# Three products ahead of RWKV-7's recurrent rounds, made by GpSimd instead of VectorE

## The reference, cut to what matters

```
def wkv7_scan(r, w, k, v, kk, a):
    def step(state, xs_t):
        r_t, w_t, k_t, v_t, kk_t, a_t = xs_t
        sa = jnp.einsum('bhvk,bhk->bhv', state, -kk_t)
        state = (state * w_t[:, :, None, :] + sa[..., None] * (kk_t * a_t)[:, :, None, :]
                 + v_t[..., None] * k_t[:, :, None, :])
        return state, jnp.einsum('bhvk,bhk->bhv', state, r_t)
...
def rwkv7_group(p, mu, w0, w2, a0, a2, g2, k_k, k_a, r_k, ln_w, ln_b):
...
    y = wkv7_scan(r_h, heads(decay), k_h, v_h, kk, heads(a))
...
    bonus = jnp.sum(r_h * k_h * r_k, axis=-1, keepdims=True) * v_h
    return (y + bonus.reshape(b, s, RW_WIDTH)) * gate
```

## Time and profile before

| | |
|---|---|
| median of 3 executions | 2797.43 us (2796.68 to 2800.03) |
| the profiled execution | 2797.85 us, of which the span of the trace is 2796.0 us |
| PE, PEld busy | 2748.7 us (98%), 2380.8 us (85%) |
| DVE busy | 1913.8 us (68%) |
| ACT busy | 1399.0 us (50%) |
| POOL busy | 106.9 us (4%) |
| granted TensorE clock, mean | 0.998 |

### The profile page before, as it was taken

How to read it: one execution, slowest core, us unless ns; L and a number is a source line. 1 busy time by engine, 2 the same in 40 slices (tenths; PEclk the granted TensorE clock), 3 DMA queues, 4 the chain that set the end, 5 groups by cost and what they waited for, 6 DMA issues and landing times.

```text
span 2796.0 us, 46874 instructions
## 1 busy us (share of the span) xinstructions
PE 2748.7 (98%) x17930; PEld 2380.8 (85%) x17930; DVE 1913.8 (68%) x2378; ACT 1399.0 (50%) x1805; POOL 106.9 (4%) x122
## 2 busy tenths in 40 slices
PE   9999999999999999999999999989999999999998
PEld 8888888888888888888887888788988888888886
DVE  7898887768656556566687665955876566575664
ACT  6545557566434444344567545635664344344444
POOL 0000000151000000000000000030200000000000
PEclk9999999999999999999999999999999999999999
DMA  7555554766666665665465444402645666656654
GB/s 245 184 184 181 158 171 154 231 194 195 190 194 188 192 192 188 195 188 190 150 194 160 128 129 121 147 22 96 198 153 184 198 190 188 195 187 191 192 188 151
DMA packets 415239, 487.83 MB, mean 174 GB/s; under 512 B 14961, under 2 KB 346737, under 8 KB 415073
## 3 DMA queue, kind: packets, MB, share of 16 engines
q1 hardware_dynamic: 413216, 478.55, 54.7%
q0 software_dynamic: 1856, 6.98, 0.7%
HBM read 482.33 MB, written 3.15 MB: 174 GB/s over the span
## 4 chain that ended last, share of the span: by engine, by line
PE 89%; DVE 6%; ACT 3%; issue 2%; DMA 0%; ACTq 0%; SPq 0%; DVEq 0%
PE pg L514 36%; PE pg L521 20%; PE pg L465 17%; PE pg L470 8%; DVE lo L370 1%; PE pg L476 1%; DVE work L924 1%; ACT hi L329 1%; PE p L1687 1%; PE p L1988 1%; DVE xa L782 0%; PE p L2001 0%; DVE dnc L1354 0%; PE p L1243 0%; DVE work L902 0%
## 5 line engine op out<-in xcount | busy, mean ns | idle before, releaser
L370 DVE TENSOR_TENSOR lo<-raw,hi 128x1024 fp32r<-128x1024 f32 x895 | 1081.9, 1228 | 683.9 <-ACT hi L329 680.3
L329 ACT ACTIVATE hi<-raw 128x1024 fp32r<-128x1024 f32 (+1 forms) x894 | 935.6, 1056 | 1118.7 <-PE pg L521 654.3
L514 PE MATMUL pg<-xa,hi 128*128 128x512 f32 x4144 | 1048.1, 395 | 2.4 <-DVE work L417 1.0
L514 PEld LDWEIGHTS pg<-xa,hi 128*128 128x128 f32 x4144 | 745.8, 189 | 140.6 <-issue 2.0
L521 PEld LDWEIGHTS pg<-xa,lo 128*128 128x128 f32 x4208 | 573.3, 190 | 50.0 <-DVE lo L370 10.0
L521 PE MATMUL pg<-xa,lo 128*128 128x256 f32 x4208 | 588.5, 283 | 4.7 <-DVE lo L370 4.7
L465 PE MATMUL pg<-hi,xb 128*128 128x512 f32 x2048 | 506.0, 389 | 0.0
L465 PEld LDWEIGHTS pg<-hi,xb 128*128 128x128 f32 x2048 | 383.9, 188 | 79.4
L470 PE MATMUL pg<-lo,xb 128*128 128x512 f32 x1024 | 273.7, 389 | 0.0
L470 PEld LDWEIGHTS pg<-lo,xb 128*128 128x128 f32 x1024 | 192.2, 188 | 39.9
L514 PE MATMUL pg<-xb,hi 128*128 128x512 f32 x896 | 226.1, 394 | 0.1
(11 more groups left out here) (428 smaller groups left out, 1673.3 us busy)
## 6 DMA issues: line engine op xcount, KB each, us to landing
raw<-w_in SPq DMA_DIRECT2D x264, 512.0 KB, 4.5
raw<-ffn_w SPq DMA_DIRECT2D x256, 512.0 KB, 3.8
raw<-w_up SPq DMA_DIRECT2D x128, 512.0 KB, 3.9
raw<-w_down SPq DMA_DIRECT2D x128, 512.0 KB, 4.5
raw<-w_o SPq DMA_DIRECT2D x32, 512.0 KB, 4.8
raw<-w_out SPq DMA_DIRECT2D x32, 512.0 KB, 4.6
raw<-w_sb_out SPq DMA_DIRECT2D x16, 512.0 KB, 4.9
raw<-w_conv_out SPq DMA_DIRECT2D x16, 512.0 KB, 4.7
```

The source lines that it names most:

```text
L329: nc.scalar.activation(hi[:, slot, :, 0:g.tiles * P], raw[:, slot, :, 0:g.tiles * P], ACT.Copy).then_inc(hi_ready, 1)
L370: nc.vector.tensor_tensor(lo[:, slot, :, wide_], raw[:, slot, :, wide_], hi[:, slot, :, wide_].bitcast(F32), ALU.subtract).then_inc(lo_rea ...
L514: nc.tensor.matmul(pg[:, par, t, :], lhsT=hi[:, slot, k, c:c + P], rhs=g.x[:, kk, :], start=(j == 0 and k == 0), stop=False)
```

## The change

Three DVE instructions become POOL instructions with the same operands: alpha, rho (both 128 x 2048) and bn (128 x 1536). They stand in a new function `rwp_pool`, ahead of `rw_pool(pool, 0)` in POOL's program. alpha waits for "ba" and for ep; rho waits for "beta" too, since it overwrites what beta reads; bn waits for the summed bonus and for the third block of v. The readers wait for POOL instead: PE before the product `mat(pe, "ba", 0)`, DVE before it copies masks (`rw_cut`) over a part of ep, and DVE in the last round before it adds to bn. The steps of DVE beside the other slabs stay where they are.

```
@@ rwp_pe
             RP.act.wait(pe, "kt")
+            RP.pool.wait(pe, "rho")
             mat(pe, "ba", 0)
@@ rwp_dve
-            RP.act.wait(dve, "ep")
             RP.dve.wait(dve, "ba")
-            RP.dve.done(nc.vector.tensor_tensor(jc(rw_ar[:, 0]), jc(rw_kk[:, :, :]), ctok(rw_ep, 0), ALU.mult), "alpha")
+            RP.act.wait(dve, "em")
             yield
             RP.dve.done(nc.vector.tensor_tensor(jc(rw_beta[:, :, :]), jc(rw_a[:, :, :]), ctok(rw_em, 1), ALU.mult), "beta")
...
+            RP.act.wait(dve, "ep")
             dve_link(nc.vector.tensor_tensor(fac, rw_ep[:, 0:16:2, P], rw_em[:, 1:16:2, 0], ALU.mult))
...
-            RP.dve.done(nc.vector.tensor_tensor(jc(rw_ar[:, 1]), jc(rw_r), ctok(rw_ep, 1), ALU.mult), "rho")
             yield from skip(6)
-            RP.act.wait(dve, "bonus")
-            dve.wait_ge(v_shifted, 3)
-            RP.dve.done(nc.vector.tensor_tensor(rw_bn[:, 0:6], rw_bn[:, 0:6], rw_v[:, 0:6], ALU.mult), "bn")
+            RP.pool.wait(dve, "rho")
+        def rwp_pool(pool):
+            RP.dve.wait(pool, "ba")
+            RP.act.wait(pool, "ep")
+            RP.pool.done(nc.gpsimd.tensor_tensor(jc(rw_ar[:, 0]), jc(rw_kk[:, :, :]), ctok(rw_ep, 0), ALU.mult), "alpha")
+            pool.wait_ge(r_shifted, 4)
+            RP.dve.wait(pool, "beta")
+            RP.pool.done(nc.gpsimd.tensor_tensor(jc(rw_ar[:, 1]), jc(rw_r), ctok(rw_ep, 1), ALU.mult), "rho")
+            RP.act.wait(pool, "bonus")
+            pool.wait_ge(v_shifted, 3)
+            RP.pool.done(nc.gpsimd.tensor_tensor(rw_bn[:, 0:6], rw_bn[:, 0:6], rw_v[:, 0:6], ALU.mult), "bn")
```

More of the change, by code:

```diff
@@ L1742, in build_program @@
         RP = Trio("rwp", ["wa0", "wa1", "kk", "bonus", "bt", "vt01", "vt23", "b2"],
-                  ["scan0", "scan1", "sc", "k", "kk", "ba", "alpha", "beta", "bonus", "kappa", "rho", "bn", "bn3"],
+                  ["scan0", "scan1", "sc", "k", "kk", "ba", "beta", "bonus", "kappa", "bn3"],
                   ["tanh", "wa0", "wa1", "kkr", "sq", "kf", "max", "ln", "root", "em", "ep", "bonus", "bt", "kt", "vt01",
-                   "vt23", "b2", "k2"])
+                   "vt23", "b2", "k2"], ["alpha", "rho", "bn"])
         lora_in = sem("lora_in")
@@ L2221, in rw_pe @@
             if not r:
-                RP.dve.wait(pe, "rho")
+                RP.pool.wait(pe, "rho")
             beside = tail_pe(pe, r - 1) if r else beside_first_pe(pe)
@@ L2356, in rw_dve @@
                 state_dve(dve, r, 2)
+                RP.pool.wait(dve, "bn")
                 for j in range(8):
@@ L2628, in _ @@
                 pool.dma_start(rw_lw[h][64:P, :], a["rw_a2_2"][:, 512 * h:512 * h + 512]).then_inc(lora_in, 16)
+            rwp_pool(pool)
             for r in range(4):
```

## The result

| | before | changed |
|---|---|---|
| median | 2797.72 us (2794.67 to 2800.03, 15 executions) | 2802.89 us (2800.56 to 2806.57, 15 executions) |
| span of the profiled execution | 2796.0 us | 2800.7 us |
| ratio | | 1.0021, 95% interval 1.0013 to 1.0028 |

The changed kernel is 5.2 us slower in the median, 5.9 us by the ratio. The forecast was 2804.1 us, 6.7 us slower than the 2797.4 us that the prediction started from.

What follows compares the result with a forecast made beforehand. DVE was taken to bound the 25.3 us stretch after 1785.7, PE the rest. Terms 1.6 + 4.5 - 0.3 + 0.9 = 6.7 us slower gave a median of 2804.1 us, range 2799.5 to 2808.5.

Steps and rivals of the forecast that it cites:

- low end: Lower edge of the forecast's own range, 2803.0 us: holds of 4.2 us and the clock staying up.
- The bound: In the 25.3 us after 1785.7, DVE's gapless chain sets PE's pace; alpha and rho off it would gain 2.5 us.
- The hold: POOL's alpha and rho each keep DVE's two-SBUF-input instructions (L425, first L1916) waiting 4.5 us; L422, reading PSUM, runs.
- The sum: Whole kernel: L425 1.6, rho's hold 4.5, rho's step -0.3, clock 0.9, together 6.7 us slower.
- Rho's own step: Rho's 2.20 us leave DVE behind the chain's last split, shortening only PE's next wait: 0.3 us gained.
- The clock: PE's idle before its matmuls of 1800.13 grows from 1.25 to 5.8 us, and the granted clock falls: 0.9 us.
- third rival: POOL gets in one instruction earlier, with a second long idle for the clock: 2804.8 to 2806.5 us; 12%.
- bn: Ahead of round 0, DVE's 4.3 us of idle time covers POOL's bn hold of at most 3.4 us: nothing.
- DVE isn't held: Rival: DVE runs beside POOL's products and its chain gets 2.5 us shorter, 2794.9 us; 15%.
- POOL gets its turn only in part: Rival: alpha holds DVE, but rho waits for a gap in DVE's work; 1.3 us slower, 2798.7, up to 2801.5; 15%.
- One instruction earlier: Rival: POOL's alpha goes ahead of the split of 1784.78, costing 2.3 instead of 1.6 us, 2804.8 to 2806.5; 12%.
- POOL is slower on these tiles: Rival: ep is read in pieces of 128 columns, the examples in 256, so POOL takes longer: 2806 to 2809.5 us; 8%.

Runs made afterwards that it cites:

- alpha alone: Only the alpha product on POOL, rho and bn left on DVE, against the kernel before: 2797.94 against 2797.52 us, ratio 1.0003; stretch from kk to round 0 +1.08 us.
- The fills: Against the changed kernel, POOL fills the places of alpha and rho with zeros, bn on DVE: 2794.01 us, kernel before 2797.52; stretch -2.39 us.
- late order on DVE: Against the kernel before, alpha and rho stay on DVE but five and one steps later, nothing moved to POOL: 2795.23 against 2797.26 us; stretch -2.38 us.
- late on POOL: Against the changed kernel, alpha on POOL waits for the last split of g_rv, bn on DVE: 2801.53 us, kernel before 2797.26; stretch +2.54 us.
- rho alone: Only the rho product on POOL, alpha and bn left on DVE, against the kernel before: 2803.90 against 2797.52 us, ratio 1.0021; stretch +5.52 us.
- eight pieces: Against the changed kernel, alpha and rho each as eight POOL instructions of 256 columns, bn on DVE: 2804.35 us, kernel before 2797.26; stretch +5.69 us.
- late on DVE once more: Repeat of the kernel with alpha and rho later on DVE, against the kernel before: 2795.53 against 2797.80 us, ratio 0.9993; stretch -2.39 us.
- POOL multiplies by zero: Against the changed kernel, POOL multiplies kk and kk*a by zero, one SBUF input, bn on DVE: 2803.31 us, kernel before 2797.80; stretch +4.53 us.

## Why the prediction was right

The forecast was right in its mechanism and too high in its size. The measured 2802.89 us lies just under its own range, 2803.0 to 2806.0, inside the range of 2799.5 to 2808.5. By the prediction's own terms that low end (holds of 4.2 us, no fall of the clock) is 1.3 + 4.2 - 0.3 = 5.2 us, 2802.6 from a median of 2797.4; 2803.0 comes out only from the profiled execution's 2797.85. No run shows a hold of 4.2 us: alpha's was 4.0 and rho's 3.96 in the changed kernel. And the 5.2 us of the median came about otherwise than at that low end: with shorter holds and with a fall.

- *The bound*. Right: what is put into DVE's chain ahead of 1803.67 moved PE one for one (L425's delay of 1.07 us gave +1.08 with alpha alone). The fills (-2.39) and the late order on DVE (-2.38) give the 2.5 us that I had worked out for taking alpha and rho off.
- *The hold*. Right in kind, with who is held and who is not: L422 ran, L425 and the first L1916 stood, each behind one split. Its size was off: 4.0 us measured against 4.5. I had taken the rate from two operations of 1024 columns, 2.35 ns a column; alpha took 5.10 - 0.97 = 4.13 us net of its wait behind the split (1784.43 to 1785.40), 2.0 ns a column; in the run late on POOL, where it had no split to wait for, it took 4.20. Both are under my 4.8.
- *The sum*, term by term: L425 moved PE's block start by 1.06 us (11.41 us after kk's start instead of 10.35; forecast 1.6), rho's hold 3.96 (4.5), the clock +0.74 (0.9): the second L521 starts 30.19 us after kk's start instead of 24.43, which is 5.76 us. Rho's own step gave 0.3 of it back behind that (-0.3). Together 5.46 us; forecast 6.7. Of the 1.2 us between the two, the holds are 1.1 and the clock 0.2.
- *The clock*. No run shows the 0.9 us that stands in the sum for it. The runs showed 0.74 us at rho's wait in the changed kernel and 1.74 with rho alone and with eight pieces; the trace of before has a fall behind an idle of 2.01 us, where eight matmuls took 3.28 us instead of 2.00 to 2.11. The fall at rho's wait came where it was forecast. The one behind L425's wait of 2.01 us was not in the sum (the prediction has a second fall only under its third rival); it cost nothing. That the price of 0.9 us was near is in part luck: with rho alone and with eight pieces the wait at this place (5.20 and 4.69 us) came with a fall of about twice the length (the clock 0.57 over 8 us and 0.50 over 6), and it cost 1.74 us.
- *bn* at nothing: right, measured alone, 0.01 us. The hold was 3.3 us (at most 3.4 forecast). What it left of DVE's idle time was 0.97 us.
- *The rivals*. "DVE isn't held" and "POOL gets its turn only in part" fell with L425 and L1916. "One instruction earlier" did not come: the split began 0.16 us ahead of alpha. "POOL is slower on these tiles" was wrong the other way.

That POOL's reading of SBUF and not POOL's activity as such holds DVE is what these runs show: POOL's fill of 1.81 us didn't hold (L1916 at 3.25 us), a POOL instruction with one SBUF input did (L425 3.42 us for 0.69). On DVE's side L422, with a PSUM input, took its 0.68 us beside alpha, while the copies L1932, with one input in SBUF and none in PSUM, took 0.67 us for 0.19 in the median. Why they were held no view shows. No copy stood beside alpha or rho in the changed kernel, so its sum isn't touched.

Open is why a fall of the clock lasts some 3.5 us in one execution (the two falls of the changed kernel) and 7 or 10 in another. These lengths are estimates, what the windows' granted clock lacks to 1.00, divided by 0.50. With it go the rounds: the seven profiles in which the clock was down for no more than some 3.5 us in them have 86.8 to 88.1 us, the other six, with 4 to 8 us by the same estimate, 89.0 to 90.8. And with it go the executions of one kernel: of the changed kernel's 15, the three above 2805 us are those with a mean granted clock of 0.995, the rest have 0.996 to 0.998.

## What to carry to other kernels

- Work given to GpSimd held VectorE in this kernel: instructions with two tiles in SBUF stood while GpSimd read two tiles (L425 3.97 us for 0.69, the eight L1916 7.21 for 3.25) or one (3.42 and 6.63), and small copies with one tile were held as well (0.67 us for 0.19). L422, with an input in PSUM, was not (0.68). A product of 2.2 us on VectorE became a hold of 4.0 us. It was free only where VectorE had that much time to give, as bn showed (3.3 us held, the stretch unchanged to 0.01), and eight smaller pieces took 6.3 us from VectorE for 7.2.
- Before moving work to another engine, look where the same engine has idle time later: alpha and rho, five steps and one step later on VectorE, gave what GpSimd was meant to give.
- Where an engine's chain sets the pace for a few slabs, measure the change in that stretch of the profile. Two profiles of one kernel differed there by 0.01 us (late on DVE) and by 0.21 (changed, with falls of the clock in the stretch); the median is good to some 2 us. But a profile's other stages say nothing of the median: the rounds took 86.8 to 88.1 us in seven profiles and 89.0 to 90.8 in the six with the longer falls of the clock.

## What was not expected of the hardware

- GpSimd's `tensor_scalar` with one input of 128 x 2048 float32 is shown with 6.28 us, of which 0.96 are the wait behind a split, longer than the product of two tiles (5.10, of which 0.97 are wait). It held VectorE for 3.4 us only. The duration shown for GpSimd was thus not the length of the hold.
- GpSimd's fill of the same tile took 1.81 us.
- A fall of the clock didn't always follow one and the same idle time. The fall of the delta-rule stage around 1550 us (0.54 from 1550 to 1552) came in 7 of the 13 profiles (before, changed, alpha alone, rho alone, late on POOL, late on DVE once more, POOL multiplies by zero) and not in the other 6 (with eight pieces the clock fell some 14 us later instead), though that stage is the same code in all and PE's idle time before it was 2.00 to 2.02 us in all 13. Where it came, PE's next wait ended 15.4 us after the idle time, where it didn't, 13.9: it cost 1.5 us. The profile of before is one of those that paid it, so comparing whole spans would have credited the six others with it.
